# Last expert's context units behind its latents, and three result tiles added by DMA, in a diffusion step with mixture of experts

## What is computed

```python
def expert_choice_ffn(h, w_router, w_gate, w_up, w_down):
    ...
    vals, idx = lax.top_k(aff.T, cap)      # 16 experts; cap = 128 latents, 16 context tokens
    xs = hf[idx]
    hid = silu(xs @ w_gate) * (xs @ w_up)
    out = (hid @ w_down) * vals[..., None]
    y = zeros_like(hf).at[idx.reshape(-1)].add(out.reshape(-1, d))

    f = expert_choice_ffn(h, ...)
    x = x + g2 * rmsnorm(f, n_post_ffn)    # context and latents have their own g2
```

## Time and profile before

| | |
|---|---|
| median of 3 runs | 2093.1 us (2091.38 to 2095.25) |
| the profiled execution's own time | 2092.53 us |
| its span | 2090.8 us |
| TensorE busy | 2000.4 us, 96% |
| VectorE busy | 1183.1 us, 57% |
| ScalarE busy | 743.6 us, 36% |
| GpSimd busy | 234.1 us, 11% |
| mean granted clock of TensorE | 0.982 |

### The profile page before, as it was taken

One profiled execution on the slowest core, in us unless ns is written; L12 is line 12 of the kernel. 1 busy time (PEld: TensorE's weight loads), 2 busy tenths in 40 slices (PEclk: granted clock), 3 DMA queues, 4 the chain that ended last, 5 costly groups with the idle time before them and its releaser, 6 DMA issues.

```text
span 2090.8 us, 32779 instructions
## 1 busy us (share of the span) xinstructions
PE 2000.4 (96%) x12759; PEld 1731.3 (83%) x12759; DVE 1183.1 (57%) x1623; ACT 743.6 (36%) x840; POOL 234.1 (11%) x241
## 2 busy tenths in 40 slices
PE   6999999999999999999999995899999999999992
PEld 4898989889999999999999885687777777777772
DVE  5654646475554232322122656877777777777765
ACT  7622222131111111111111332465566556556552
POOL 1010101010000000000000123111211111121102
PEclk9999999999999999999999997999999999999996
DMA  9011102224443111112223747758887788888768
GB/s 334 20 50 46 53 33 75 78 61 144 143 143 113 41 40 40 40 50 74 85 85 133 272 143 295 302 190 320 313 314 276 283 321 319 319 308 311 266 254 314
DMA packets 179509, 365.95 MB, mean 175 GB/s; under 512 B 10500, under 2 KB 99532, under 8 KB 178564
## 3 DMA queue, kind: packets, MB, share of 16 engines
q1 hardware_dynamic: 162736, 311.23, 41.0%
q0 software_dynamic: 16624, 54.04, 8.5%
q10 hardware_dynamic: 100, 0.03, 0.0%
HBM read 322.24 MB, written 43.02 MB: 175 GB/s over the span
## 4 chain that ended last, share of the span: by engine, by line
PE 89%; DVE 4%; issue 4%; DMA 2%; ACT 1%; POOL 0%; SPq 0%; DVEq 0%; POOLq 0%; ACTq 0%
PE ps L919 11%; PE ps L920 11%; PE ps L921 11%; PE ps L1190 8%; PE ps L1192 8%; PE ps L1199 8%; PE ps L1208 8%; PE ps L941 3%; PE ps L942 3%; PE ps L943 3%; PE ps L1122 2%; PE ps L1124 1%; PE ps L1123 1%; PE ps L990 1%; PE ps L991 1%
## 5 line engine op out<-in xcount | busy, mean ns | idle before, releaser
L2159 DVE TENSOR_TENSOR e_lo<-raw,e_hi 128x2048 fp32r<-128x2048 f32 x192 | 439.4, 2290 | 89.4 <-ACT e_hi L1611 89.4
L1611 ACT CAST e_hi<-raw 128x2048 fp32r<-128x2048 f32 x192 | 367.2, 1914 | 211.4 <-PE ps L1199 211.4
L919 PE MATMUL ps<-h_hi,w_hi 128*128 128x384 f32 x936 | 313.7, 335 | 0.2 <-DVE w_lo L1728 0.2
L921 PE MATMUL ps<-h_hi,w_lo 128*128 128x384 f32 x936 | 312.8, 334 | 0.0
L920 PE MATMUL ps<-h_lo,w_hi 128*128 128x384 f32 x936 | 312.8, 334 | 0.0
L1728 DVE TENSOR_TENSOR w_lo<-w_raw,w_hi 128x1024 fp32r<-128x1024 f32 x64 | 78.0, 1218 | 209.5 <-ACT w_hi L1341 209.4
L919 PEld LDWEIGHTS ps<-h_hi,w_hi 128*128 128x128 f32 x936 | 175.8, 188 | 8.0 <-issue 4.3
L920 PEld LDWEIGHTS ps<-h_lo,w_hi 128*128 128x128 f32 x936 | 175.8, 188 | 0.0
L921 PEld LDWEIGHTS ps<-h_hi,w_lo 128*128 128x128 f32 x936 | 175.8, 188 | 0.0
L1190 PE MATMUL ps<-e_hi,x_hi 128*128 128x512 f32 x512 | 159.6, 393 | 0.2 <-ACT x_hi L1617 0.2
L1192 PE MATMUL ps<-e_lo,x_hi 128*128 128x512 f32 x512 | 157.7, 389 | 0.0
(11 more groups left out here) (287 smaller groups left out, 3305.6 us busy)
## 6 DMA issues: line engine op xcount, KB each, us to landing
raw<-in_w_gate_dram SPq DMA_DIRECT2D x64, 1024.0 KB, 8.4
raw<-in_w_up_dram SPq DMA_DIRECT2D x64, 1024.0 KB, 13.6
raw<-in_w_down_dram SPq DMA_DIRECT2D x64, 1024.0 KB, 12.4
w_raw<-in_w_in_dram SPq DMA_DIRECT2D x48, 512.0 KB, 4.0
ada_k<-in_w_ada_dram SPq DMA_DIRECT2D x64, 256.0 KB, 2.8
merged_d<-merged POOLq DMA_DIRECT2D x16, 576.0 KB, 3.6
ada<-in_w_ada_dram SPq DMA_DIRECT2D x7, 1024.0 KB, 15.8
ret_part<-merged_d POOLq DMA_DIRECT2D x8, 576.0 KB, 4.0
```

Of the source, the lines that this page charges most:

```text
L919: pe.matmul(out, w_hi[:, slot, k, :], xh, start=(k == 0), stop=False)
L921: mm = pe.matmul(out, w_lo[:, slot, k, :], xh, start=False, stop=(k == KD - 1))
L1611: act.copy(e_hi[u % 4][:].rearrange("p k n -> p (k n)"), raw[(u + 8) % 12][:].rearrange("p k n -> p (k n)"))\
L2159: dve.tensor_tensor(e_lo[u % 4][:].rearrange("p k n -> p (k n)"), raw[(u + 8) % 12][:].rearrange("p k n -> p (k n)"), e_hi[u % 4][:].rearr ...
```

## The change

1. In expert 15 TensorE does only context units 0 and 1 before it turns the hidden rows; units 2 to 7 come behind the latents of units 8 to 11. gate_context (ScalarE) and hidden_context (VectorE) move behind them.
2. g2 lies over x_hi and x_lo now, norm_ffn over xg_l, sq3 over hid. Each table is loaded when its own place is free; x1_lat comes in two halves (behind context units 1 and 3), x1_ctx between the loads of f_all.
3. For n = 3, 4, 5 (tiles 4, 5, 6; BY_DMA) SyncE copies x1_d to the output, DRAM to DRAM. VectorE only weighs them, ScalarE scales them by the deviation (`scale_y`), and GpSimd adds them onto the output by a DMA that sums, behind all of its `rstd` groups. VectorE's order is now LAST_STEPS, with 15 operations where there were 18.

The diff, without the declarations of semaphores:

```diff
 LAST_GROUPS = [(0, 1), (1, 1), (2, 2), (4, 2), (6, 3)]
+BY_DMA = (3, 4, 5)
+LAST_STEPS = "w0 w1 f0 w2 f1 w3 f2 w4 w5 w6 w7 w8 f6 f7 f8".split()
+LAST_FINISHED = [int(s[1:]) for s in LAST_STEPS if s[0] == "f"]
 LAST_GROUP_OF = [g for g, (n, count) in enumerate(LAST_GROUPS) for _ in range(count)]
...
         x1_ctx = at("x1_ctx", 0, [P, D])
-        g2 = at("g2", SL, [P, 2, D])
-        norm_ffn = at("norm_ffn", 3 * SL, [P, D])
+        g2 = at("g2", A_DECAY, [P, 2, D])
+        norm_ffn = at("norm_ffn", Z + 16 * SL, [P, D])
         y_all = at("y_all", 4 * SL, [P, NT, D])
         f_all = at("f_all", Z, [P, NT, D])
-        sq3 = at("sq3", Z + 16 * SL, [P, D])
+        sq3 = at("sq3", A_S, [P, D])
         def aff_of(n):
...
+            sp.wait_ge(xg_turned, 2 * EXPERTS)
+            sp.dma_start(norm_ffn[:], n_post_ffn[0:1, :].broadcast_to([P, D])).then_inc(norm_ffn_in, 16)
+            sp.wait_ge(lat_used, 12 * (EXPERTS - 1) + 8)
+            for j in range(2):
+                sp.dma_start(g2[:, j, :], mod_d[j:j + 1, R_G2 * D:(R_G2 + 1) * D].broadcast_to([P, D])).then_inc(g2_in, 16)
             for b in range(2):
                 sp.wait_ge(x1_stored[b], 16 * (5 - b))
-            sp.wait_ge(raw_used, 12 * (EXPERTS - 1) + 8)
-            for j in range(2):
-                sp.dma_start(g2[:, j, :], mod_d[j:j + 1, R_G2 * D:(R_G2 + 1) * D].broadcast_to([P, D])).then_inc(g2_in, 16)
-            sp.dma_start(norm_ffn[:], n_post_ffn[0:1, :].broadcast_to([P, D])).then_inc(norm_ffn_in, 16)
-            sp.dma_start(x1_ctx[:], x1_d[0]).then_inc(x1_landed, 16)
-            sp.dma_start(x1_lat[:], x1_d[1:NT].rearrange("t p d -> p t d")).then_inc(x1_landed, 16)
+            for n in BY_DMA:
+                sp.dma_start(ys[LAST_ORDER[n] - 1], x1_d[LAST_ORDER[n]]).then_inc(y_based, 16)
+            sp.wait_ge(raw_used, 12 * (EXPERTS - 1) + 2)
+            sp.dma_start(x1_lat[:, 0:4, :], x1_d[1:5].rearrange("t p d -> p t d")).then_inc(x1_landed, 16)
+            sp.wait_ge(raw_used, 12 * (EXPERTS - 1) + 4)
+            sp.dma_start(x1_lat[:, 4:8, :], x1_d[5:NT].rearrange("t p d -> p t d")).then_inc(x1_landed, 16)
             sp.wait_ge(added_l, 16 * EXPERTS)
...
                 if t == 0:
+                    sp.wait_ge(raw_used, 12 * (EXPERTS - 1) + 6)
+                    sp.dma_start(x1_ctx[:], x1_d[0]).then_inc(x1_ctx_landed, 16)
                     sp.wait_ge(added_c, 16 * EXPERTS)
...
                   .then_inc(f_in_s[n % 3], 16)
-            for n, t in enumerate(LAST_ORDER):
+            for n, done in enumerate(LAST_FINISHED):
+                t = LAST_ORDER[done]
                 sp.wait_ge(y_ready, n + 1)
                 sp.dma_start(ys[t - 1] if t else yp, y_all[:, t, :]).then_inc(y_stored, 16)
-            sp.wait_ge(y_stored, 16 * NT)
+            sp.wait_ge(y_stored, 16 * len(LAST_FINISHED))
+            sp.wait_ge(y_added, 16 * len(BY_DMA))
         @block.gpsimd
...
                 rstd(f_rs[:, ts], f_ms[:, ts], rms_eps[:, ts]).then_inc(f_rstd, 1)
+            pool.wait_ge(y_based, 16 * len(BY_DMA))
+            for j, n in enumerate(BY_DMA):
+                pool.wait_ge(y_scaled, j + 1)
+                pool.dma_start(ys[LAST_ORDER[n] - 1], y_all[:, LAST_ORDER[n], :], accum_op=ALU.add).then_inc(y_added, 16)
             pool.wait_ge(state_stored, 32 * PAIRS)
...
                     latent(e, u, 2, x_hi, x_lo)
+                def context_in(units):
+                    for u in units:
+                        if u == 4:
+                            pe.wait_ge(out_ready, 2 * e)
+                        context(u, 4 if u < 4 else 7, 0 if u < 4 else CAP_Q, xc)
                 if not first:
                     pe.wait_ge(xc_turned, e + 1)
-                    for u in range(4):
-                        context(u, 4, 0, xc)
-                    pe.wait_ge(out_ready, 2 * e)
-                    for u in range(4, 8):
-                        context(u, 7, CAP_Q, xc)
+                    context_in(range(2 if last else 8))
                 for half in range(2):
...
                     latent(e, u, 5, hT_hi, hT_lo, hT_lo_done)
+                if last:
+                    context_in(range(2, 8))
                 if not first:
...
                     high(e, u)
-                if not first:
+                if not first and not last:
                     gate_context(e)
...
                     act.copy(hT_hi[:, 4 * half:4 * half + 4, :].rearrange("p k n -> p (k n)"), ps[:, half, :]).then_inc(hT_hi_done, 1)
+                if last:
+                    gate_context(e)
                 if not last:
...
             expert(EXPERTS - 1, True)
-            for n, t in enumerate(LAST_ORDER):
-                load = LAST_LOAD_OF[n]
+            def square_f(n):
+                load, t = LAST_LOAD_OF[n], LAST_ORDER[n]
                 act.wait_ge(f_in_s[load % 3], 16 * (load // 3 + 1))
...
                 act.activation(sq3[:], f_all[:, t, :], ACT.Square, scale=D ** -0.5, accum_out=f_ms[:, n:n + 1]).then_inc(f_sq, 1)
+            def scale_y(n):
+                t = LAST_ORDER[n]
+                act.wait_ge(y_weighed, BY_DMA.index(n) + 1)
+                act.wait_ge(f_rstd, LAST_GROUP_OF[n] + 1)
+                act.activation(y_all[:, t, :], y_all[:, t, :], ACT.Copy, scale=f_rs[:, n:n + 1]).then_inc(y_scaled, 1)
+            for n in range(6):
+                square_f(n)
+            scale_y(3)
+            square_f(6)
+            square_f(7)
+            scale_y(4)
+            square_f(8)
+            scale_y(5)
         @block.vector
...
                     dve.tensor_tensor(hs, ps[:, 2 + half, :], hs, ALU.mult).then_inc(hid_done, 1)
-                if not first:
+                if not first and not last:
                     hidden_context(e, 3)
...
                                   ALU.mult).then_inc(out_ready, 1)
+                if last:
+                    hidden_context(e, 3)
                 dve.wait_ge(raw_used, 12 * e + 12)
...
                 dve.wait_ge(f_in_s[load % 3], 16 * (load // 3 + 1))
-                if t:
+                if n in BY_DMA:
+                    dve.tensor_tensor(y_all[:, t, :], f_all[:, t, :], g2[:, 1, :], ALU.mult).then_inc(y_weighed, 1)
+                elif t:
                     did(dve.tensor_tensor(y_all[:, t, :], f_all[:, t, :], g2[:, 1, :], ALU.mult))
...
                 dve.wait_ge(f_rstd, LAST_GROUP_OF[n] + 1)
+                if t == 0:
+                    dve.wait_ge(x1_ctx_landed, 16)
                 dve.scalar_tensor_tensor(y_all[:, t, :], y_all[:, t, :], f_rs[:, n:n + 1], x1_lat[:, t - 1, :] if t else x1_ctx[:],
                                          ALU.mult, ALU.add).then_inc(y_ready, 1)
-            for n in range(NT):
-                weigh_ffn(n)
-                if n >= 2:
-                    finish(n - 2)
-            finish(NT - 2)
-            finish(NT - 1)
+            for step in LAST_STEPS:
+                (weigh_ffn if step[0] == "w" else finish)(int(step[1:]))
 # ---- launch: one core; inputs and outputs as the reference has them ----
```

More of the change, by code:

```diff
@@ L460, in build @@
         g2_in = sem("g2_in")
-        x1_landed = sem("x1_landed")
+        x1_landed, x1_ctx_landed = sem("x1_landed"), sem("x1_ctx_landed")
         f_in_s = [sem(f"f_in_s{g}") for g in range(3)]
@@ L464, in build @@
         y_ready, y_stored = sem("y_ready"), sem("y_stored")
+        y_based, y_weighed, y_scaled, y_added = sem("y_based"), sem("y_weighed"), sem("y_scaled"), sem("y_added")
         m_rstd, x1_rstd, gn_var, gn_rstd = sem("m_rstd"), sem("x1_rstd"), sem("gn_var"), sem("gn_rstd")
```

## The result

The changed kernel takes 2099.6 us (median of 8 runs), the kernel before 2092.7: a ratio of 1.003, 95% interval 1.0021 to 1.0039. I had forecast 2094.3 and most likely no difference; it is slower by 0.3%, within the range by 0.4 us and on the side to which I gave 0.19. The profiled execution has a span of 2099.2, where before had 2090.8; at 2100.9 us it is 1.4 slower than the median of the runs, so the profiles differ by 8.4 where the medians differ by 6.9.

The account below looks back on a forecast made before the run. The prediction took the end to be bound by TensorE, then the latents' scatter, then the final norm. Scatter landing at 2056.3 plus 35.7 made a span of 2092.0, hence a time of 2094.3 us; range 2086 to 2100.

Parts of the forecast that it names:

- The most likely case: Whole kernel: gain before the scatter's landing given back by late sums; 2094.3 us, own range 2090 to 2098, chance 0.43.
- case 4: Final sums: latencies add up, landings about 4.1 apart, end at A' + 40.9; 2099.5 us, chance 0.09.
- case 6: Last expert: moved context units bring nothing because something else holds the hidden rows; 2099.1 us, chance 0.03.
- The side "slower": Whole kernel: outcomes slower than before by over 0.2%, from three rival cases; chance 0.19 together.
- Part 1: Last expert on TensorE: six context units moved behind the latents start the turning 4.8 us earlier; context's later scatter costs 0.7.
- Part 2: Moved loads and residual copies: copies hidden, latents' scatter takes 9.1 us (6.2 to 10.0), x1_lat's second half 5.2.
- case 5: Residual copies: slow DRAM to DRAM transfers push x1_lat's first half into the scatter and f_all loads; 2102 us, chance 0.07.
- Part 3: Final norm: deviation at A' + 21.4, then the sums and stores, ending at A' + 35.7.
- A': Landing of the latents' scatter in the last expert of the new kernel, forecast at 2056.3 us, a gain of 4.8.
- case 7: Final sums: they wait for VectorE's finishes, starting at A' + 25.0; 2095.3 us, chance 0.03.
- The sum: Whole span: scatter landing 2056.3 plus 35.7 behind it gives 2092.0 against 2090.8, + 1.2 us.
- case 2: Final sums: hidden beside the stores, VectorE's last store ends the span at A' + 28.3; 2086.9 us, chance 0.27.

Follow-up runs that it names:

- e8_four_no_sums: Changed kernel with no tile added by DMA and context units 0 to 3 ahead of the turning: 2088.5 us, ratio 0.9971 against before.
- e11_loads_alone: Kernel before with only the changed kernel's loads; all eight context units first, no sums, no copies: 2091.3 us, ratio 0.9986 against before.
- e7_sums_early: Changed kernel with GpSimd issuing the sums ahead of the last group's deviation, tile n = 5 scaled before the ninth square: 2094.9 us, ratio 1.0001 against before.
- e1_no_sums: Changed kernel with no tile added by DMA; VectorE finishes all nine tiles, no copies of residuals: 2092.9 us, ratio 0.9993 against before.
- e3_four_units: Changed kernel with context units 0 to 3, not only 0 and 1, ahead of the turning: 2098.5 us, ratio 1.0015 against before.
- e10_four_early: Changed kernel with sums issued ahead of the last group's deviation and context units 0 to 3 ahead of the turning: 2091.8 us, ratio 0.9985 against before.

## Why the prediction was right or wrong

That the time lies in the range is in part luck. The most likely case had a range of its own that ended at 2098; 2100 was in the range for the prices of cases 4 and 6, and neither of them made the time. The side "slower" came true by none of its three cases.

**Part 1** was right in size (4.8, with the wait of 0.4 for hid), and context's scatter landed in time. The moved units were not quite free: from the scatter's landing to the end e8_four_no_sums takes 30.6 and e11_loads_alone 29.7, and the forecast had 0.7 for this.

**Part 2** failed at the step that priced the scatter: "The nearest row is its own, 9.1. Both ends are kept: 6.2 (a gain of 2.9) and 10.0". It took 11.4, 2.3 over the term and 1.4 over the bound. With x1_lat's second half issued 13 us or more ahead of it, it takes 6.1 to 6.9 in five kernels, so the row of before already held about 3 us of such a cost. I took the row of before as the nearest, but in before the load had been running for 12 us; the move tied half of x1_lat to context unit 3, which now ends as the scatter is issued. Of the 4.8 us from part 1, the scatter took 2.3 back against before; against what the loads alone give, 5.2. The same step said of that half of x1_lat "it needs 5.2 beside the scatter"; it took 11.8, was still landing 0.8 after the scatter, and put the first square 4.8 behind the landing where before had 3.8. Why a transfer issued 0.3 us behind the scatter holds it up more than one that has run for 12 us (9.1) is not settled; in an early stretch of 2 us the engines moved only 143 GB/s at a share of 0.76:

```profile
2049.00:2051.00 2.00, 2.00 (x44) 1.23 (x40) 0.00 (x0) 0.00 (x0) 0.79 (x1) 1.00 0.76 143
```

The copies from DRAM to DRAM landed in 7.0 to 9.3, all by 2043.4 and so ahead of the scatter (case 5 fell).

**Part 3** was right in its times up to the last landing: deviation at A' + 21.2 (forecast 21.4; its power took 0.85 with VectorE idle, not 2.9), last finish at A' + 25.0, first sum 5.2 behind its issue, SyncE past its waits at A' + 35.6 (forecast 35.7). That a sum takes 2.6 of all engines fits: 3 x 2.6 + 3 x 1.3 = 11.7 is the 12 us stretch at 0.99 and 252 GB/s. The order within it was another. I had the sums land 2.6 apart and the stores' 3.9 in a term of its own; the sums landed 4.5 and 3.9 apart, as each shared the engines with a store, and the last landing was a store. A spacing of about 4.1 was what case 4 (latencies that add) was to be told by, so that sign came; its price of A' + 40.9 did not, since the engines were full, and it fell. Case 7 (sums that wait for VectorE) fell too: the first sum landed at A' + 26.4, where that case has A' + 30.2. The rule that case 7 takes from the Trainium skill (SBUF — State Buffer, "A bandwidth-pool intuition that's wrong") did not bind here: the first sum was issued as VectorE's finishes began and landed 5.2 later, as one with nothing beside it was estimated to.

**The sum** failed where it took A' + 35.7, the last landing, for the end: it has no term for GpSimd's end, 3.8 us. That and the scatter's 2.3 are 6.1 of the 7.2 between the forecast span of 2092.0 and the measured 2099.2; 0.9 is the later start of the whole expert, and 0.2 are left for the rest. Case 2, which I gave 0.27, could not have come true as priced: with the last issue of GpSimd at A' + 24, its DRAIN would have ended at A' + 31.6 or later, 3.3 over the A' + 28.3 of that case. The trace of before has the rows for this; I did not ask what the engines do behind their last instruction.

## What to carry to other kernels

Ask of each engine when its last instruction may be issued, not only which result lands last: GpSimd needs 7.6 us behind its own and 4.6 behind the landing of its last transfer, and a kernel whose end looks like SyncE's may be within half a microsecond of GpSimd's. When a load is freed from one wait, look at what its new wait coincides with; a 2 MB load issued just behind the one transfer that everything waits for took back half of what moving the matmuls had won (2.3 of 4.8 us). And a sum by DMA costs the DMA engines twice a store, and GpSimd has to issue it; issued early, the three sums cost SyncE's last wait only 0.2 to 0.6 us, and GpSimd's end another 1.2.

## What the runs showed of the hardware

- GpSimd's closing DRAIN ends 7.6 to 7.7 us behind its last instruction (7622 ns behind a memset, with no transfer near), or 4.5 to 4.7 behind the landing of its own last transfer, summing or plain, whichever is later (14 profiles). ScalarE's and VectorE's DRAINs took 0.2 to 3.6, SyncE's 7 ns.
- A transfer that sums moves some 205 GB/s at full share (211 at 1.07 in e7_sums_early, 2080 to 2082), a plain one 400 to 410 (408 in e1_no_sums, 2087 to 2089); in 12 us of a mix, 252.
- The scatter of 0.5 MB took 6.1 to 6.9 with no load beside it or with one that was ending (1.0 MB of it left in e3_four_units, 0.8 in e10_four_early), 8.2 with 0.5 MB issued 0.3 behind it, 11.4 to 11.8 with 2 MB issued 0.3 to 0.4 behind it.
